# Memory keys and values kept on chip through the experts, and memory weights and rows loaded in longer runs

## The chip, the cores and the metric

The kernel runs on one core of one Trainium2 chip. A core has TensorE (matrix products), VectorE, ScalarE, GpSimd and SyncE, which here only issues loads, and 16 DMA engines that all queues share. The metric is the device time of one execution in microseconds (us), the median of the runs.

## The reference, cut to what matters

A first block (attention, a recurrent mixer, then a mixture of 32 experts) is followed by a second block of two layers on 256 tokens of width 1024. Both layers of the second block have attention over 256 memory rows, whose keys and values depend on inputs alone, not on the tokens:

```python
def memory_attention(qm, mem, w_mem_kv):
    B, M, _ = mem.shape
    km, vm = jnp.split(mem @ w_mem_kv, 2, axis=-1)
    km = km.reshape(B, M, MEM_HEADS, MEM_HEAD_DIM)
    vm = vm.reshape(B, M, MEM_HEADS, MEM_HEAD_DIM)
    lg = jnp.einsum('bshd,bmhd->bhsm', qm, km).astype(jnp.float32) * (MEM_HEAD_DIM ** -0.5)
    p = jax.nn.softmax(lg, axis=-1)
    o = jnp.einsum('bhsm,bmhd->bshd', p, vm)
    return o.reshape(qm.shape[0], qm.shape[1], MEM_W).astype(qm.dtype)
```

`mem` is 256 x 1024 and `w_mem_kv` 1024 x 512 for each layer, all in float32. Every expert has a gate and an up matrix of 1024 x 512 and a down matrix of 512 x 1024, 2 MB each. The kernel runs all 32 experts.

## The kernel before, in words

**Stages.** The first block's attention and mixer come first, then the router, then the experts, in 16 pairs (`DUOS`); then the first block's final normalization, the second block's first attention and FFN, and its second attention and FFN. The engines run programs of their own and meet at semaphores.

**The experts' loads.** A pair needs six units of 2 MB: two gate, two up, two down. Even pairs use the six slots of `ring`. Odd pairs use four spare places for gate and up (`spare`: one in `wide_rows` and `rowvec`, three in `arena`) and the ring for down. SyncE issues them in the order of use. Before each it waits until the unit's last reader is done (`used_up`: `moe["gate_up"]` or `moe["down"]`). An expert's unit is read in runs of 16 KB for each partition, or 8 KB where a unit comes in halves. Several loads are queued at a time.

**The memory's part.** Between the pairs, the keys and values of both layers are made. SyncE loads one memory weight matrix per layer (`mem_weights`, in the place of a gate unit: `mem_unit`) and the memory rows into `X`. TensorE turns the rows in 16 transposes (`mem_columns`, line 945), ScalarE puts them back into `X` as `memT` (line 2128), and TensorE makes keys and values (`mem_product`, through `product`, line 886) in banks 2 and 3, at 289 us for the first layer and 354 us for the second. Two gate loads, of pairs 4 and 6, go where the matrices lay and wait for these products (`first_unit_swapped`, line 807).

**Where the products go.** Their place in the second block, `km` and `vm`, is the end of `arena_and_mem`, which a spare unit uses until the last pair. So ScalarE copies each 512-column product in three pieces (`mem_out`, line 2136) into free places (`mem_stage`: 256 columns in `w_router`, 128 in `tri`, 128 in `wide_rows`), and GpSimd stores each piece to a tensor in device memory, `by_memory` (line 3153): 12 stores of 64 or 128 KB, 1 MB in all. The next product isn't copied until the stores of the one before have landed (`mem_stored`). After the last gate and up product SyncE loads all 1 MB into `km` and `vm` in one piece (line 863), between the loads of the second block's first weights; `mem_back` tells TensorE that they are there, before the memory's scores (line 1481).

**The end of the experts.** The last pair's units come in halves. The last product of gate and up (line 1242) is followed by ScalarE's silu (line 2108), VectorE's product (line 2669), transposes, and the down products (line 1260), the second half of which waits for the last load. VectorE then copies the result (line 2672), TensorE adds it (line 1269), ScalarE squares (line 2179), and VectorE normalizes into `X` (lines 2776 to 2780). TensorE turns `X` and ScalarE empties it into `wide_rows` (line 2091). `keep_awake` (line 892) issues products of zeros that write a bank nobody reads.

**After that.** SyncE loads in the order of `ring_units`: from the second block two parts of the attention input, then the stored products, then the third part, two compression matrices and the rest. Line 1671 and 1853 are the attention's products, line 1695 and 1745 the FFNs'. GpSimd makes sums for the FFNs (lines 3182 to 3187).

Of the kernel before, what the change touches and what calls it, by code (L numbers as in the profile page):

```python
# [14 lines left out]
F32 = mybir.dt.float32  # L15
# [7 lines left out]
P = 128  # L23
T = 256
# [247 lines left out]
def build(nc, x, meta_tokens, lb_logits, g_mix, w_in, sb_gain, hg_gain, w_out, g_ffn, w_router_group,  # L272
# [9 lines left out]
    with ExitStack() as ctx:  # L282
# [3 lines left out]
        def sem(name):  # L286
            return ctx.enter_context(nc.semaphore(name))
# [39 lines left out]
        def take(n, *dims):  # L327
# [99 lines left out]
        by_block = nc.dram_tensor("by_block", [HEADS, CMP_PAD, T], F32).ap()  # L427
        by_memory = nc.dram_tensor("by_memory", [P, UNIT // 2], F32).ap()
        mem_stage = [(0, MEM, w_router[:, :, :].rearrange("p k n -> p (k n)")[:, 0:MEM]), (MEM, P, tri[:, :]),
                     (MEM + P, P, wide_rows[:, 0:P])]  # L430
        expanded = sem("expanded")
# [6 lines left out]
        mem_in, mem_weights_in, mem_turned, mem_kept = sem("mem_in"), sem("mem_weights_in"), sem("mem_turned"), sem("mem_kept")  # L438
        mem_made, mem_staged, mem_stored, mem_back = sem("mem_made"), sem("mem_staged"), sem("mem_stored"), sem("mem_back")
        in_pack, in_pack1 = sem("in_pack"), sem("in_pack1")  # L440
# [191 lines left out]
        def _(sp):  # L632
# [96 lines left out]
            def used_up(u, pairs):  # L729
                sp.wait_ge(moe["down" if u >= 4 else "gate_up"], pairs * 2)  # L730
# [57 lines left out]
            def mem_weights(layer):  # L788

                used_up(0, 2 * layer + 2)  # L790
                src = kmaj((a_w_mem_kv_2, b_w_mem_kv_2)[layer][0])
                sp.dma_start(mem_unit(layer), src).then_inc(mem_weights_in, 16)

            mem_weights(0)
            for u in range(SPARES, 6):
                used_up(u, 2)
                next_unit(u, 2, False)
            sp.dma_start(X[:, :, :], mem_2[0].rearrange("(b p) d -> p b d", p=P)).then_inc(mem_in, 16)

# [59 lines left out]
            for u in (2, 1):  # L859
                load(second + u)  # L860
            used_up(1, DUOS)
            sp.wait_ge(mem_stored, 16 * 3 * 4)
            sp.dma_start(arena_and_mem[:, ARENA:ARENA + half_unit], by_memory).then_inc(mem_back, 16)
            for u in (0, 3, 4, 6, 9):
# [11 lines left out]
        def _(pe):  # L876
# [61 lines left out]
            def mem_columns():  # L938
                pe.wait_ge(mem_in, 16)
                for j in range(4):  # L940
                    if j >= 2:
                        pe.wait_ge(mem_kept, j - 1)
                    for r in range(2):
                        for tb in range(TB):
                            last = pe.transpose(bank[2 + j % 2][:, r * T + tb * P:r * T + (tb + 1) * P],
                                                X[:, tb, (2 * j + r) * P:(2 * j + r + 1) * P], ident[:, :])
                    last.then_inc(mem_turned, 1)
# [493 lines left out]
            def attend(layer):  # L1441
# [17 lines left out]
                def scores(together):  # L1459

                    _, kind, pair, _, _ = att[together[0]]
                    if kind == "mem":
                        wait_emptied(pe, "b_qm" if layer else "a_qm")
                        pe.wait_ge(mem_back, 16)
                    else:
                        wait_emptied(pe, "b_q" if layer else "a_q", pair // 2)
                        wait_emptied(pe, *(("b_k", pair // 2) if layer else ("a_kv", 1)))
# [429 lines left out]
        def _(act):  # L1897
# [233 lines left out]
            def mem_out(n):  # L2131
                act.wait_ge(mem_made, n + 1)
                if n:
                    act.wait_ge(mem_stored, 16 * 3 * n)
                for at, w, v in mem_stage:
                    last = act.activation(v, bank[2 + n % 2][:, at:at + w], ACT.Copy)
                last.then_inc(mem_staged, 1)
# [15 lines left out]
            for layer in range(2):  # L2153
                moe_quad(1 + layer, memory=layer)
            act.wait_ge(mem_stored, 16 * 3 * 4)
            with act.Fori(3, LAST_QUAD) as i:
# [27 lines left out]
            def empty_ln(name, layer, which):  # L2184
                at = PACK_ROWS + layer * LAYER_ROWS
                empty_normed(name, at + LAYER_PACK[f"ln{which}_g"][0], at + LAYER_PACK[f"ln{which}_b"][0], 2 * layer + which - 1)

            empty_normed("xTa", cols[:, PACK["g_final"][0]:PACK["g_final"][0] + KT], None)
            def attend(layer):
# [125 lines left out]
        def _(dve):  # L2315
# [458 lines left out]
            for tb in range(TB):  # L2774
                dve.wait_ge(y_squared, tb + 1)
                ts(sm(10 + tb, 1), sm(604 + 2 * tb, 1), 1.0 / D, EPS, ALU.mult, ALU.add).then_inc(stat_ready, 1)
                dve.wait_ge(sq_ready, 5 + 2 * tb)
                step(dve.reciprocal(sm(12 + tb, 1), sm(12 + tb, 1)))
                for n in range(2):
                    last = ts(X[:, tb, n * HALF:(n + 1) * HALF], bank[4 + 2 * tb + n][:, :], sm(12 + tb, 1), None, ALU.mult)  # L2780
                last.then_inc(normed, 1)
# [282 lines left out]
        def _(pool):  # L3064
# [82 lines left out]

            for n in range(4):
                layer, side = divmod(n, 2)
                pool.wait_ge(mem_staged, n + 1)  # L3150
                for at, w, v in mem_stage:
                    to = (2 * side + layer) * HALF + at
                    pool.dma_start(by_memory[:, to:to + w], v).then_inc(mem_stored, 16)
            pool.wait_ge(moe["down"], 2 * DUOS)
# [101 lines left out]
```

## Time and profile before

| what | value |
|---|---|
| median of 3 runs | 1387.59 us (1387.23 to 1391.06) |
| profiled execution, from first to last instruction | 1388.4 us |
| TensorE busy | 1219.2 us, 88% |
| VectorE, ScalarE, GpSimd busy | 469.4, 269.5, 327.3 us |
| moved by DMA | 337.94 MB, mean 243 GB/s |
| chain that ended last: TensorE, DMA | 71%, 18% |
| experts, first saturated load to last down product | about 237 to 675.6 us |
| granted clock of TensorE, mean | 0.942 |

The page gives one execution. Its span is all of it that the profile shows; no time outside the span is given. Busy shares are over the whole span; a stage with another limit has to be read by itself, in the stretches below. The chain goes back from the last instruction to what released it. "DMA share" is the mean busy share of the 16 engines, which can read slightly over 1 in a short stretch.

### The profile page before, as it was taken

Reading aid. Unit: us, or ns where it says so; the run is one execution under the profiler, and the core shown is the slowest. Engines: PE = TensorE matmul, PEld = TensorE weight load, DVE = VectorE, ACT = ScalarE, POOL = GpSimd, SP = SyncE. Lnnn points to the kernel's source line nnn. Section 1 sums busy time; section 2 is a strip of 40 time slices with the busy share of each in tenths; the row PEclk is TensorE's granted clock in tenths of the full one; section 3 lists DMA queues with packets and bytes.
Section 4 is the critical chain, followed back from the end, with each engine's and each line's share of the span. In section 5 each row is a group of like instructions: output and inputs, shape, how many; then the busy total and the mean of one; then the engine's idle time right before and its main releaser. Section 6 shows DMA issues by size and latency. Waiting matters only on the chain.

```text
span 1388.4 us, 18557 instructions
## 1 busy us (share of the span) xinstructions
PE 1219.2 (88%) x7567; PEld 795.4 (57%) x7567; DVE 469.4 (34%) x1160; ACT 269.5 (19%) x692; POOL 327.3 (24%) x348
## 2 busy tenths in 40 slices
PE   7999999985956566676898989999999999999997
PEld 6774555352512122231476559999448665999843
DVE  3352434101001010110213646444574214534467
ACT  4313432010000000000224532111003322111100
POOL 5000100000000000000100336878200113878800
PEclk9999999998978778888999999999999999999999
DMA  9643346999999999999984306544434038555400
GB/s 345 190 173 120 121 163 263 409 427 422 427 429 428 427 428 429 430 426 422 400 283 157 104 2 224 183 170 182 151 122 152 1 118 284 191 166 183 152 1 30
DMA packets 103102, 337.94 MB, mean 243 GB/s; under 512 B 6936, under 2 KB 58448, under 8 KB 88813
## 3 DMA queue, kind: packets, MB, share of 16 engines
q1 hardware_dynamic: 99958, 327.38, 61.3%
q0 software_dynamic: 2864, 9.35, 1.8%
q8 instruction: 59, 0.97, 0.3%
q14 instruction: 22, 0.18, 0.0%
q10 hardware_dynamic: 199, 0.06, 0.0%
HBM read 334.63 MB, written 3.91 MB: 244 GB/s over the span
## 4 chain that ended last, share of the span: by engine, by line
PE 71%; DMA 18%; DVE 4%; POOL 3%; ACT 2%; issue 2%; SPq 1%; POOLq 0%; DVEq 0%; ACTq 0%
PE bank L1695 18%; PE bank L886 17%; DMA ring<-in_w_expert_up 10%; PE bank L1745 8%; PE bank L1242 5%; PE bank L1260 4%; DMA ring<-in_w_expert_down 2%; DMA ring<-in_w_expert_gate 2%; DMA wide_rows<-in_w_expert_gate 2%; PE bank L1853 2%; PE bank L1132 2%; PE bank L1671 2%; PE bank L1521 1%; PE bank L1578 1%; PE bank L1269 1%
## 5 line engine op out<-in xcount | busy, mean ns | idle before, releaser
L886 PE MATMUL bank<-wide_rows,ring 128*128 128x256 f32 (+3 forms) x576 | 129.4, 377 | 1.9 <-DVE arena L2423 1.7
L1695 PE MATMUL bank<-R,arena 128*128 128x128 f32 x1056 | 125.1, 275 | 0.0
L1242 PE MATMUL bank<-ring,arena 128*32 128x512 f32 x512 | 77.6, 695 | 50.5 <-DMA ring<-in_w_expert_up 38.0
L1695 PEld LDWEIGHTS bank<-R,arena 128*128 128x128 f32 x1056 | 121.5, 192 | 0.0
L886 PEld LDWEIGHTS bank<-wide_rows,ring 128*128 128x128 f32 (+1 forms) x576 | 106.5, 193 | 23.0 <-issue 6.4
L1242 PE MATMUL bank<-wide_rows,arena 128*32 128x512 f32 x128 | 68.8, 689 | 49.1 <-DMA arena<-in_w_expert_up 36.2
L2669 DVE TENSOR_TENSOR arena<-arena,bank 64x512 f32<-64x512 f32 x16 | 11.1, 692 | 295.4 <-ACT arena L2108 295.4
L1695 PE MATMUL bank<-wide_rows,ring 128*128 128x128 f32 x704 | 91.2, 275 | 1.5 <-ACT wide_rows L2093 1.5
L1695 PEld LDWEIGHTS bank<-wide_rows,ring 128*128 128x128 f32 x704 | 84.7, 192 | 2.5 <-ACT wide_rows L2093 2.5
L1260 PE MATMUL bank<-ring,arena 128*32 128x512 f32 x504 | 72.5, 718 | 13.6 <-ACT arena L2111 10.1
L1745 PE MATMUL bank<-arena 128*128 128x512 f32 x176 | 81.4, 593 | 0.5 <-DVE arena L3032 0.5
L3171 POOL TENSOR_TENSOR arena<-arena,small 128x512 f32<-128x512 f32 (+1 forms) x44 | 38.0, 865 | 182.0 <-DVE small L2853 144.5
L1242 PEld LDWEIGHTS bank<-ring,arena 128*32 128x32 f32 x512 | 19.4, 126 | 98.3 <-issue 84.4
L3182 POOL TENSOR_TENSOR arena<-ring 128x512 f32<-128x512 f32 x44 | 56.6, 1286 | 77.2 <-PE bank L1695 56.9
L2108 ACT ACTIVATE arena<-bank 64x512 f32<-64x512 f32 x16 | 9.4, 588 | 329.1 <-PE bank L1242 329.1
L3146 POOL DMA_DIRECT2D wide_rows<-in_g_final x1 | 0.5, 538 | 304.1 <-PE bank L1260 304.1
L886 PE MATMUL bank<-ring,wide_rows 128*128 128x512 f32 (+2 forms) x192 | 71.8, 529 | 0.0
L1242 PEld LDWEIGHTS bank<-wide_rows,arena 128*32 128x32 f32 x128 | 14.7, 124 | 96.8 <-issue 80.4
L1242 PE MATMUL bank<-arena 128*32 128x512 f32 x384 | 67.0, 668 | 0.0
L1745 PE MATMUL bank<-ring,arena 128*128 128x512 f32 x132 | 62.4, 594 | 1.0 <-POOL arena L3209 1.0
L2999 DVE TENSOR_TENSOR arena<-arena,bank 128x128 f32<-128x128 f32 x44 | 12.6, 287 | 135.6 <-ACT arena L2273 135.6
L1745 PEld LDWEIGHTS bank<-arena 128*128 128x128 f32 x176 | 33.2, 190 | 42.9 <-issue 40.7
(383 smaller groups left out, 1990.3 us busy)
## 6 DMA issues: line engine op xcount, KB each, us to landing
ring<-in_w_expert_down SPq DMA_DIRECT2D x29, 2048.0 KB, 16.8
ring<-in_ffn_w_in SPq DMA_DIRECT2D x44, 1024.0 KB, 8.4
ring<-in_w_expert_gate SPq DMA_DIRECT2D x16, 2048.0 KB, 25.0
ring<-in_w_expert_up SPq DMA_DIRECT2D x16, 2048.0 KB, 33.1
arena<-in_w_expert_up SPq DMA_DIRECT2D x14, 2048.0 KB, 30.9
ring<-in_ffn_w_out SPq DMA_DIRECT2D x10, 2048.0 KB, 8.0
ring<-in_w_in SPq DMA_DIRECT2D x7, 2048.0 KB, 15.6
arena<-in_w_expert_gate SPq DMA_DIRECT2D x7, 2048.0 KB, 26.5
```

What stands on the lines that cost most here:

```text
L886: last = pe.matmul(dst, lhsT, rhs, start=k == 0, stop=k == len(pairs) - 1)
L1132: last = pe.matmul(b[:, :], mixT[:, k, tb * P:(tb + 1) * P], w[:, k, :], start=k == 0, stop=k == KT - 1)
L1242: last = pe.matmul(bank[e % 2][at:at + SLOTS, :], xg_tile(e % 2, k)[:, SLOTS * r:SLOTS * r + SLOTS], w[r][:, kk, :], start=k == 0, stop=k ...
L1260: last = pe.matmul(bank[e % 2][at:at + SLOTS, :], hidden_T[e % 2][:, f * DUO + SLOTS * r:f * DUO + SLOTS * (r + 1)], w[r][:, ff, n * HALF: ...
L1269: last = pe.matmul(bank[4 + 2 * tb + n][:, :], give[e % 2][half, tb * P:(tb + 1) * P], yrow[e % 2][half, :], start=False, stop=final)
L1521: last = pe.matmul(dst, v, p, start=k == 0, stop=k == len(lower[1]) - 1)
L1671: last = pe.matmul(b[:, :], headT[:, k, tb * P:(tb + 1) * P], w[:, k, :], start=k == PAIRS, stop=k == PAIRS - 1)
L1695: last = pe.matmul(up_banks[layer][u % 4][i][:, at * P:(at + 1) * P], weights(k), columns(k), start=k == 0, stop=k == KT // 2 - 1)
L1745: return pe.matmul(down_banks[layer][which][:, :], left, right, start=p == 0, stop=p == STEPS_F - 1)
L1853: last = pe.matmul(b[:, :], headT[:, k, tb * P:(tb + 1) * P], w[:, k, :], start=k == b_first[0], stop=k == b_last[-1])
L3171: pool.tensor_tensor(v, v, sm(684 + 8 * (u % LOGITS), 2).unsqueeze(2).broadcast_to([P, 2, w]), ALU.mult).then_inc(at_p, 1)
L3182: pool.tensor_tensor(s[0], b_low, b_high, ALU.add).then_inc(ph["w_sums"], 1)
```

## The change

1. The products stay on chip. `by_memory`, its 12 stores, its load and the semaphore `mem_stored` are gone. The first layer's products are staged by ScalarE in `w_router` and `ones` (keys) and in `tri`, `wide_rows` and `level_mask` (values), which nothing reads any more. The second layer's products go, in one instruction each and when both are made, into the first half of `X`, where `memT` is then no longer needed.
2. After the last gate and up product GpSimd copies all of it into `km` and `vm`, in seven copies of 256, 256, 512, 128, 128, 256 and 512 columns. `mem_back` is now set by the last of them. VectorE waits for it before the final normalization writes `X`, ScalarE before it writes `wide_rows`, TensorE before the memory's scores.
3. SyncE's waits for `used_up(1, DUOS)` and `mem_stored` are gone with the load.
4. Each partition gets two neighbouring rows of a memory weight matrix, 4 KB in one run instead of 2 KB, and two neighbouring memory rows, 8 KB instead of 4 KB. The transposes read every second column to match.

```diff
-        by_memory = nc.dram_tensor("by_memory", [P, UNIT // 2], F32).ap()
-        mem_stage = [(0, MEM, w_router[:, :, :].rearrange("p k n -> p (k n)")[:, 0:MEM]), (MEM, P, tri[:, :]),
-                     (MEM + P, P, wide_rows[:, 0:P])]
+        late_memory = X[:, 0, :].rearrange("p (a b c) -> p a b c", b=2, c=MEM)
+        mem_stage = [[(0, MEM, w_router[:, :, :].rearrange("p k n -> p (k n)")[:, 0:MEM]), (MEM, MEM, ones[:, 0:MEM])],
+                     [(0, P, tri[:, :]), (P, P, wide_rows[:, 0:P]),
+                      (MEM, MEM, level_mask[:, :, :].rearrange("p a b -> p (a b)").bitcast(F32))]]
...
                 used_up(0, 2 * layer + 2)
-                src = kmaj((a_w_mem_kv_2, b_w_mem_kv_2)[layer][0])
-                sp.dma_start(mem_unit(layer), src).then_inc(mem_weights_in, 16)
+                src = (a_w_mem_kv_2, b_w_mem_kv_2)[layer][0].rearrange("(j p r) n -> p j (r n)", p=P, r=2)
+                sp.dma_start(mem_unit(layer).rearrange("p (j r) n -> p j (r n)", r=2), src).then_inc(mem_weights_in, 16)
...
-            sp.dma_start(X[:, :, :], mem_2[0].rearrange("(b p) d -> p b d", p=P)).then_inc(mem_in, 16)
+            sp.dma_start(X[:, :, :], mem_2[0].rearrange("(p b) d -> p b d", p=P)).then_inc(mem_in, 16)
...
             for u in (2, 1):
                 load(second + u)
-            used_up(1, DUOS)
-            sp.wait_ge(mem_stored, 16 * 3 * 4)
-            sp.dma_start(arena_and_mem[:, ARENA:ARENA + half_unit], by_memory).then_inc(mem_back, 16)
             for u in (0, 3, 4, 6, 9):
                 load(second + u)
...
                         for tb in range(TB):
-                            last = pe.transpose(bank[2 + j % 2][:, r * T + tb * P:r * T + (tb + 1) * P],
-                                                X[:, tb, (2 * j + r) * P:(2 * j + r + 1) * P], ident[:, :])
+                            by_row = X[:, tb, j * MEM:(j + 1) * MEM].rearrange("p (f r) -> p r f", r=2)
+                            last = pe.transpose(bank[2 + j % 2][:, r * T + tb * P:r * T + (tb + 1) * P], by_row[:, r, :], ident[:, :])
...
-                        pe.wait_ge(mem_back, 16)
+                        pe.wait_ge(mem_back, 1)
...
             def mem_out(n):
-                act.wait_ge(mem_made, n + 1)
-                if n:
-                    act.wait_ge(mem_stored, 16 * 3 * n)
-                for at, w, v in mem_stage:
-                    last = act.activation(v, bank[2 + n % 2][:, at:at + w], ACT.Copy)
+                layer, side = divmod(n, 2)
+                if layer == 0:
+                    act.wait_ge(mem_made, n + 1)
+                    for at, w, v in mem_stage[side]:
+                        last = act.activation(v, bank[2 + side][:, at:at + w], ACT.Copy)
+                else:
+                    act.wait_ge(mem_made, 4)
+                    last = act.activation(late_memory[:, side], bank[2 + side][:, :].rearrange("p (b c) -> p b c", b=2), ACT.Copy)
                 last.then_inc(mem_staged, 1)
...
-            act.wait_ge(mem_stored, 16 * 3 * 4)
             with act.Fori(3, LAST_QUAD) as i:
...
+            act.wait_ge(mem_back, 1)
             empty_normed("xTa", cols[:, PACK["g_final"][0]:PACK["g_final"][0] + KT], None)
...
             for tb in range(TB):
                 dve.wait_ge(y_squared, tb + 1)
+                dve.wait_ge(mem_back, 1)
...
-            for n in range(4):
-                layer, side = divmod(n, 2)
-                pool.wait_ge(mem_staged, n + 1)
-                for at, w, v in mem_stage:
-                    to = (2 * side + layer) * HALF + at
-                    pool.dma_start(by_memory[:, to:to + w], v).then_inc(mem_stored, 16)
+            pool.wait_ge(mem_staged, 4)
+            pool.wait_ge(moe["gate_up"], 2 * DUOS)
+            for side, home in enumerate((km, vm)):
+                for at, w, v in mem_stage[side]:
+                    pool.tensor_copy(home[0].rearrange("p b c -> p (b c)")[:, at:at + w], v)
+                last = pool.tensor_copy(home[1], late_memory[:, side])
+            last.then_inc(mem_back, 1)
             pool.wait_ge(moe["down"], 2 * DUOS)
             load_rowvec(g_final)
```

## Rows read from the trace of the kernel before

**Rows 1.** Page, part 2: GpSimd and the DMA engines in 40 slices.

```profile
POOL 5000100000000000000100336878200113878800
...
DMA  9643346999999999999984306544434038555400
GB/s 345 190 173 120 121 163 263 409 427 422 427 429 428 427 428 429 430 426 422 400 283 157 104 2 224 183 170 182 151 122 152 1 118 284 191 166 183 152 1 30
```

**Rows 2.** Stretches of 237 to 675.6 us; last columns clock granted, DMA share, GB/s.

```profile
262.00:271.00 9.00, 8.46 (x72) 2.67 (x72) 1.48 (x5) 0.49 (x1) 0.00 (x0) 1.00 1.00 357
271.00:285.00 14.00, 9.43 (x66) 2.94 (x66) 0.69 (x1) 1.19 (x2) 0.00 (x0) 0.76 1.00 421
...
297.00:313.00 16.00, 15.51 (x103) 7.91 (x101) 0.00 (x0) 0.95 (x5) 3.24 (x6) 1.00 1.00 423
...
341.00:349.00 8.00, 5.53 (x44) 1.79 (x40) 0.69 (x1) 1.04 (x2) 0.00 (x0) 1.00 1.03 397
...
400.00:636.00 236.00, 149.09 (x1009) 55.40 (x1002) 20.70 (x48) 9.48 (x16) 0.00 (x0) 0.81 1.01 428
```

**Rows 3.** Waits, 237 to 676 us: total, times, longest.

```profile
PE bank L1242 <- DMA ring<-in_w_expert_up: 38.0, 4, 10.3
...
ACT w_router L2136 <- DMA by_memory<-wide_rows: 18.3, 2, 9.5
```

**Rows 4.** Chain that ended last, 237 to 420 us.

```profile
266.62 14.01 DMA ring<-in_w_expert_down
...
303.41 30.48 DMA wide_rows<-in_w_expert_gate
```

**Rows 5.** TensorE's waits for DMA from 676 us to the end.

```profile
PE bank L1260 <- DMA ring<-in_w_expert_down: 0.4, 1, 0.4
```

**Rows 6.** DMA packets in 297:313, 313:325, 361:380, 341:349 and 271:285.

```profile
q0 software_dynamic: 159, 0.39, 6.3%
...
q0 software_dynamic: 65, 0.13, 2.8%
...
q0 software_dynamic: 216, 0.52, 7.0%
...
DMA packets 1122, 3.18 MB, mean 397 GB/s; under 512 B 32, under 2 KB 32, under 8 KB 1056
...
DMA packets 600, 5.90 MB, mean 421 GB/s; under 512 B 48, under 2 KB 48, under 8 KB 304
```

**Rows 7.** Timeline of SyncE's queue, 240 to 700 us: start, length.

```profile
257.31 0.38 SPq L792 DMA_DIRECT2D wide_rows<-in_a_w_mem_kv  x1
266.25 0.80 SPq L727 DMA_DIRECT2D ring<-in_w_expert_down  x2
...
323.32 16.61 SPq L727 DMA_DIRECT2D arena<-in_w_expert_gate  x1
...
656.92 15.18 SPq L711 DMA_DIRECT2D ring<-in_a_w_in  x2
672.21 4.93 SPq L863 DMA_DIRECT2D arena<-by_memory  x1
```

**Rows 8.** GpSimd's groups by form: total, mean ns.

```profile
L3182 POOL TENSOR_TENSOR arena<-ring 128x512 f32<-128x512 f32 x44 | 56.6, 1286 | 77.2 <-PE bank L1695 56.9 <-DVE R L2866 20.3
...
L3106 POOL CAST level_mask<-arena 128x128 uint8<-128x128 f32 x7 | 2.0, 291 | 0.5
```

**Rows 9.** Timeline at the end of the experts.

```profile
669.99 0.69 DVE L2669 TENSOR_TENSOR arena<-arena,bank 64x512 f32<-64x512 f32 x1 [14.17 <-ACT arena L2108]
...
675.60 1.92 PE L1260 MATMUL bank<-ring,arena 128*32 128x512 f32 x16 [0.38 <-DMA ring<-in_w_expert_down]
...
680.23 0.15 DVE L2776 TENSOR_SCALAR small<-small 128x1 f32<-128x1 f32 x1 [1.95 <-ACT R L2179]
```

**Rows 10.** VectorE's line 2999 in the FFNs: minimum, median, maximum ns.

```profile
L2999 DVE TENSOR_TENSOR arena<-arena,bank x44: 277/288/289, 849.5 to 1312.0; 128x128 f32<-128x128 f32 x44
```

**Rows 11.** Transposes of the memory rows: minimum, median, maximum ns.

```profile
L945 PE MATMUL bank<-ident,X x16: 272/273/329, 286.1 to 288.3; 128*128 128x128 f32 x16
```

More of the change, by code:

```diff
@@ L438, in build @@
         mem_in, mem_weights_in, mem_turned, mem_kept = sem("mem_in"), sem("mem_weights_in"), sem("mem_turned"), sem("mem_kept")
-        mem_made, mem_staged, mem_stored, mem_back = sem("mem_made"), sem("mem_staged"), sem("mem_stored"), sem("mem_back")
+        mem_made, mem_staged, mem_back = sem("mem_made"), sem("mem_staged"), sem("mem_back")
         in_pack, in_pack1 = sem("in_pack"), sem("in_pack1")
```

## The prediction

> **What bounds the kernel now.** I read the page first, part 2. From the seventh to the nineteenth slice, which is where the experts are, the 16 DMA engines are 90% busy or more and move 400 to 430 GB/s [rows 1]. Cut into the experts' own stretches, the DMA share is 1.00 or a little above in every one, while TensorE is busy 149 of 236 us between 400 and 636 [rows 2]. The waits say it from the other side: in this stage TensorE waits for weights of the up matrices, 38.0 us in 4 waits on the ring alone [rows 3]. The chain of work agrees, with pieces of 14.01 and 30.48 us that are one expert load each [rows 4]. So from about 237 to 675.6 us the kernel is a stream of weights: a byte or a slow packet less in it moves the end of the experts forward, and nothing that TensorE, ScalarE or VectorE does less of in that time does. From 676 us to the end, TensorE waits for a DMA once, for 0.4 us [rows 5]. What is saved in transfers there has no price.
>
> The reader is to see where the stream is not at its plain rate. Between 400 and 636 us, experts alone, it is 428 GB/s. From 262 to 271 us it is 357, from 271 to 285 us 421, from 341 to 349 us 397 [rows 2]. The packets of those three stretches are the memory's: 1,056 of the 1,122 packets of 341 to 349 us are under 8 KB, 1,024 of them the 2 KB runs of one 2 MB memory weight matrix; in 271 to 285 us the excess is the 256 runs of 4 KB of the memory rows [rows 6].
>
> **Stores (removed).** Twelve stores on GpSimd's queue, 1 MB in all, lie inside the stream. Queue 0 took 6.3% of the 16 engines in 16 us, 2.8% in 12 us and 7.0% in 19 us [rows 6]: 1.01 + 0.34 + 1.33 = 2.68 us of the whole stream. By bytes it is (0.39 + 0.13 + 0.52) MB over 428 GB/s = 2.43 us. I take 2.6 us, ends 2.43 and 2.68. All of it counts, because loads are queued before and behind it. ScalarE's 18.3 us of waiting for the stores [rows 3] also goes, and counts for nothing: it stands under a TensorE that waits for loads afterwards.
>
> **Longer runs (changed).** The weight matrices go from 2 KB to 4 KB runs, the rows from 4 KB to 8 KB. The second matrix costs 8 us x (428 - 397)/428 = 0.58 us over the plain rate, with 1,024 packets. With 512 packets it is half, 0.29 us, if a packet has one fixed cost; the memory rows, whose 256 packets of 4 KB cost 14 us x (428 - 421)/428 = 0.23 us, say 0.46 us for 512 of 4 KB. The saving is therefore between 0.12 and 0.29 us; I take 0.2. The memory rows save 0 to 0.23 us, I take 0.1. The first matrix has the same packets but costs 9 us x (428 - 357)/428 = 1.49 us, 0.91 us more than the second. It was issued at 257.31 us with little queued, and the next load only at 266.25 us [rows 7], when TensorE was done with the down product; the second had six loads around it. Whether longer runs mend that 0.91 us no row shows. I take half, and so 0.2 + 0.45 = 0.65 us, ends 0.12 and 1.49. If the matrix lands sooner, the down weights issued at 266.25 us, which end the 14.01 us of the chain [rows 4], land sooner by as much.
>
> The Trainium skill, page DMA: Bandwidth & Descriptors, section Specifications, asks for 512 B a transfer as the least for full rate; by that, 2 KB runs are already long enough. The trace disagrees, with 397 against 428 GB/s. By the rule the three run terms would be nothing and the sum 2.6 us; by the rows it is more.
>
> **Load back (removed).** The 1 MB load of the stored products is issued at 672.21 us [rows 7], behind the last expert load, so it is no part of the stream that ends at 675.6 us. SyncE's queue stood 4.93 us in it; the loads of the second block that follow (the third part of the attention input and the two compression matrices) start about 5 us earlier. Nothing waited for those [rows 5], so this is 0. The cover is TensorE's work on the normalized rows and on the first parts of the attention input, which had landed. SyncE is also held 16.61 us behind the second memory matrix and 15.18 us at the first loads of the second block [rows 7]; fewer packets may end the first of these, but the DMA share stays 1.0 through it, so it is 0 too.
>
> **Copies on GpSimd (added).** Seven copies at the end of the experts, after the last gate and up product: 256, 256, 512 columns and 128, 128, 256, 512. The trace has no such copy. A 128-column cast takes 291 ns, a two-source sum of 512 columns 1,286 ns [rows 8]. As upper end, with half of the sum's time for 256 columns, 2 x 0.29 + 3 x 0.65 + 2 x 1.29 = 5.1 us. They can start before VectorE's last hidden product at 669.99 us, and the first instruction that waits for them is VectorE's at 680.23 us [rows 9]: a gap of 10.2 us, so 5.1 us are hidden. Behind that instruction stand the final normalization, TensorE's transposes and the whole second block, so beyond 10.2 us each us costs one. The two other waits (ScalarE's emptying into wide_rows, TensorE's memory scores) come later still. GpSimd has no other work: its next load, the final gain, waits for the last down product anyhow.
>
> VectorE's hidden product at 669.99 us now runs beside these copies. If it had to stand behind one, the last down half would be late by at most 1.29 - 0.38 = 0.9 us, 0.38 us being TensorE's idle time there [rows 9]. Against it: line 2999 has the same operands, one in the arena and one in a bank, and took 277 to 289 ns in 44 executions in the FFNs, where GpSimd is 70 to 90% busy with sums [rows 1, 10]. I take 0.
>
> **Moved and reordered.** The second layer's two products are copied out of their banks in one instruction each instead of three, the first of them only when both are made, about 7 us later. What waits for it is the gather, behind the pair's gate and up products, as before. Reading the memory rows with a step of two in the 16 transposes could make them dearer; they take 16 x 273 ns = 4.4 us by their durations [rows 11], and twice that is still inside one pair's wait, about 10 us [rows 3]. Price 0 for both.
>
> **The sum.** 2.6 + 0.2 + 0.1 + 0.65 = 3.55 us. Smallest: 2.43 + 0.12 + 0 + 0.12 = 2.67 us. The profiled span is 1388.4 us, 0.8 us above the median of the runs; nothing outside the span is shown, so the difference is taken from the median: 1387.59 - 3.55 = 1384.0 us. A measurement of this kernel tells about 0.3%, 4.2 us, from no change; the forecast lies just inside that.
>
> **Rivals.**
>
> *The stream gains more.* The memory loads run at the plain rate: 2.68 + 1.49 + 0.58 + 0.23 = 4.98 us, time 1382.6 us. For it: the first matrix's slow stretch is 2.6 times as dear as the second's with equal packets, so most of it isn't packet cost, and a shorter queue of packets may remove it. Against: the memory rows show that 4 KB packets aren't free.
>
> *Nothing is gained.* The stream is paced by when loads may be issued, not by its rate. The chain goes from TensorE's memory products into the load issued at 303.41 us [rows 4], and the one at 266.25 us too is released by TensorE. If the next buffers free no earlier, the removed stores leave gaps. The time is 1387.6 us. Against: the DMA share is 1.00 to 1.03 in every stretch [rows 2], and loads take 30 us to land, some six deep.
>
> *Slower.* GpSimd's copies hold the final normalization. They begin at 669.99 us at the latest and decide from 10.2 us on. To undo the gain they must take 10.2 + 3.55 = 13.8 us, and to be slower by over 0.3%, another 4.2 us, 17.9 us, or 2.6 us each, twice the dearest GpSimd row. The time is then above 1391.8 us.
>
> **How the numbers follow.** Forecast 0.62, more gained 0.15, nothing gained 0.15, slower or something unseen 0.08. The forecast's own range is 1382.6 to 1384.9 us, with the runs' spread on top. The 8 in 10 range is 1382.0 to 1387.8 us, which takes in the larger gain and most of no gain. Faster by over 0.3% means below 1383.4 us: 0.3 of the forecast and nearly all of the larger gain, 0.33. Slower 0.08, within 0.3% 0.59.
>
> **What would show it.** Right: queue 0 has no packets between 297 and 380 us; the last down product of the experts starts 3 to 4 us before 675.60; every later stage keeps its length; the seven copies end before VectorE's normalization; the stretch of the second memory matrix reads about 410 GB/s. Wrong: the DMA share drops below 1 near 266 or 303 us; VectorE's normalization waits for GpSimd; the time after the last down product changes; the end of the experts moves by less than 2.4 us.

## The result and the profile after

The first comparison gave 1381.33 us as the median of 7 executions (1379.6 to 1385.84) against 1388.82 us for the kernel before (7 executions, 1387.23 to 1391.66): ratio 0.9945, 95% interval 0.9927 to 0.9963. Forecast were 1384.0 us and a range of 1382.0 to 1387.8 us. So the change gained more than the range allowed. Two later comparisons on two chips, 12 executions of the changed kernel each, gave 0.9969 (0.9947 to 0.9990) and 0.9979 (0.9960 to 0.9998); the experiments below are about that difference.

The profiled execution after spans 1377.9 us and took 1379.6 us, 1.7 us more than its span; in every recorded execution it is 1.7 to 1.8 us. It is 10.5 us shorter than the profiled span before. Page, part 2, of after:

```profile
DMA  9643356999999999999974217544434048544400
GB/s 347 196 171 122 122 202 266 426 427 425 426 428 428 428 428 429 429 427 421 392 253 152 76 43 229 178 152 165 153 122 153 1 137 284 192 155 181 153 1 30
```

The stream is as full as in [rows 1]. Its slow stretches are where [rows 2] had them, some 5 to 8 us earlier and less slow. Stretches of after (busy time of the engines, then granted clock, DMA share, GB/s):

```profile
257.00:262.00 5.00, 3.76 (x36) 1.01 (x32) 0.69 (x1) 0.00 (x0) 0.00 (x0) 1.00 0.97 393
264.00:278.00 14.00, 9.46 (x63) 3.10 (x63) 0.69 (x1) 1.19 (x2) 0.00 (x0) 0.81 1.01 430
...
333.00:341.00 8.00, 5.87 (x44) 1.90 (x42) 0.69 (x1) 0.71 (x2) 0.00 (x0) 1.00 1.00 410
400.00:636.00 236.00, 149.57 (x1012) 55.78 (x1004) 20.71 (x48) 9.48 (x16) 0.00 (x0) 0.81 1.01 427
```

The second matrix, in runs of 4 KB, reads 410 GB/s in 8 us where it read 397 in runs of 2 KB, which is the figure forecast. The memory rows in runs of 8 KB read 430 against 421, but before_again reads 428 GB/s over the same work with the runs of 4 KB, so that these rates don't show a gain. The first matrix leaves a dip of 393 in 5 us where there were 357 in 9; the two windows aren't the same work, and the comparison from one starting point follows in the account of the prediction.

SyncE's queue of after, for [rows 7]:

```profile
250.62 0.38 SPq L793 DMA_DIRECT2D wide_rows<-in_a_w_mem_kv  x1
259.56 0.80 SPq L728 DMA_DIRECT2D ring<-in_w_expert_down  x2
...
317.89 0.50 SPq L728 DMA_DIRECT2D arena<-in_w_expert_gate  x1
318.44 5.38 SPq L728 DMA_DIRECT2D arena<-in_w_expert_up  x2
...
648.63 19.50 SPq L712 DMA_DIRECT2D ring<-in_a_w_in  x3
```

SyncE no longer stands 16.61 us behind the second matrix; it stands 5.38 us at a later load. The end of the experts in after, for [rows 9], with the first and the last of the seven copies:

```profile
660.66 0.40 POOL L3154 COPY arena<-w_router 128x256 f32<-128x256 f32 x1 [471.90 <-PE bank L1240]
...
661.17 0.69 DVE L2670 TENSOR_TENSOR arena<-arena,bank 64x512 f32<-64x512 f32 x1 [13.63 <-ACT arena L2106]
...
662.71 0.61 POOL L3155 COPY arena<-X 128x512 f32<-128x512 f32 x1
...
666.81 1.92 PE L1258 MATMUL bank<-ring,arena 128*32 128x512 f32 x16 [0.41 <-DMA ring<-in_w_expert_down]
...
671.44 0.15 DVE L2778 TENSOR_SCALAR small<-small 128x1 f32<-128x1 f32 x1 [1.95 <-ACT R L2179]
```

The copies run from 660.66 to 663.32 us and VectorE needs them at 671.44 us. VectorE's product beside them takes 0.69 us as before. The last down product starts at 666.81 instead of 675.60 us: 8.79 us of the 10.5 are there by then. How many of these belong to the experts? The two gate loads that open the full stream were issued at 237.80 us before and at 232.81 us after: 4.99 us were there before anything that the change touches. From that issue to the last down product it is 437.80 us before and 434.00 us after: 3.8 us. The last 1.7 us came in the second block.

The 6.7 us outside are the granted clock. Four stretches of before:

```profile
56.00:67.00 11.00, 10.70 (x39) 9.02 (x40) 0.76 (x2) 0.75 (x2) 2.46 (x3) 0.71 0.46 148
136.00:148.00 12.00, 12.00 (x42) 6.54 (x42) 2.03 (x7) 3.16 (x6) 0.00 (x0) 0.86 0.21 89
243.00:249.00 6.00, 6.00 (x40) 1.66 (x44) 0.61 (x1) 0.00 (x0) 0.00 (x0) 0.72 1.01 429
816.00:823.00 7.00, 6.79 (x32) 3.44 (x28) 0.42 (x1) 0.43 (x2) 0.68 (x1) 0.76 0.01 2
```

And where the same work is in after:

```profile
56.00:67.00 11.00, 10.99 (x58) 9.82 (x59) 2.42 (x5) 1.23 (x2) 2.46 (x3) 1.00 0.52 158
132.00:144.00 12.00, 12.00 (x54) 7.30 (x54) 2.61 (x9) 4.79 (x10) 0.00 (x0) 1.00 0.27 110
238.00:244.00 6.00, 6.00 (x56) 1.84 (x60) 0.69 (x1) 0.00 (x0) 0.00 (x0) 1.00 1.00 426
806.00:813.00 7.00, 5.72 (x34) 3.21 (x35) 0.91 (x3) 1.37 (x5) 1.69 (x2) 1.00 0.01 2
```

The clock column is 0.71, 0.86, 0.72 and 0.76 before and 1.00 in all four after: TensorE was at its lower level, 1.2 GHz, for part of each stretch. Before, the product of 32 instructions at 56 us takes 10.17 instead of 7.14 us, the one of 16 at 138 us 8.47 instead of 7.03 us, and the eight ahead of it 1.45 instead of 1.16 us: 4.8 of the 5.0 us that after is ahead when the stream begins. Around 816 us it is 5.10 instead of 3.63 us in the chain, most of the last 1.7 us. Either the change takes these drops away, or they fall by chance.

### The profile page after: what moved, and what is told of

Its sections match the earlier page's. It is cut to its first block, busy times and chain, and to the rows that moved or that the text cites. A ratio compares the mean times of both kernels' runs of the same rounds, so it can differ in the third digit from the quotient of the medians.

```text
span 1377.9 us, 18538 instructions
## 1 busy us (share of the span) xinstructions
PE 1210.1 (88%) x7559; PEld 791.4 (57%) x7567; DVE 469.1 (34%) x1160; ACT 269.0 (20%) x687; POOL 323.6 (23%) x343
## 4 chain that ended last, share of the span: by engine, by line
PE 71%; DMA 18%; DVE 4%; POOL 3%; ACT 2%; issue 2%; SPq 1%; POOLq 0%; DVEq 0%; ACTq 0%
PE bank L1693 18%; PE bank L884 17%; DMA ring<-in_w_expert_up 10%; PE bank L1743 8%; PE bank L1240 5%; PE bank L1258 3%; DMA ring<-in_w_expert_down 2%; DMA ring<-in_w_expert_gate 2%; PE bank L1851 2%; DMA wide_rows<-in_w_expert_gate 2%; PE bank L1130 2%; PE bank L1669 2%; PE bank L1519 1%; PE bank L1576 1%; PE bank L1267 1%
## 5 line engine op out<-in xcount | busy, mean ns | idle before, releaser
L884 PE MATMUL bank<-wide_rows,ring 128*128 128x256 f32 (+3 forms) x576 | 126.4, 371 | 1.9 <-DVE arena L2424 1.7
```

The lines of the kernel that those rows point to most:

```text
L884: last = pe.matmul(dst, lhsT, rhs, start=k == 0, stop=k == len(pairs) - 1)
```

## The experiments

Theory one: the change moves the experts' stretch by about 3 us and nothing else; the rest of the first 7.5 us is how the clock's drops fell in few executions. Theory two: the drops belong to the kernel before, and the change removes them too. A third reading gives the longer runs, not the stores, the larger part.

The measure for the stretch is in every profile: the issue of the two gate loads ("ring<-in_w_expert_gate x2") to the start of the last down product. The table has it, what lies ahead of it and behind it, all from one profiled execution each, and the medians of all executions of the comparison (that of before is shared by the kernels that ran on the same chip).

| kernel | ahead, us | stretch, us | behind, us | median, us (executions) | before beside it, us | ratio (interval) |
|---|---|---|---|---|---|---|
| before | 237.80 | 437.80 | 712.80 | | | |
| before_again | 238.75 | 437.00 | 711.25 | 1388.30 (12) | 1388.04 | 0.9999 (0.9983 to 1.0016) |
| before_third | 234.55 | 437.00 | 714.55 | 1386.98 (12) | 1387.91 | 0.9993 (0.9973 to 1.0012) |
| after | 232.81 | 434.00 | 711.09 | 1381.33 (7) | 1388.82 | 0.9945 (0.9927 to 0.9963) |
| after_again | 234.51 | 434.03 | 711.16 | 1384.73 (12) | 1388.18 | 0.9969 (0.9947 to 0.9990) |
| after_third | 239.22 | 433.87 | 711.01 | 1385.64 (12) | 1387.91 | 0.9979 (0.9960 to 0.9998) |
| runs_only | 234.79 | 436.18 | 709.53 | 1387.42 (12) | 1388.04 | 0.9994 (0.9978 to 1.0010) |
| onchip_only | 239.04 | 435.74 | 709.52 | 1384.95 (12) | 1388.04 | 0.9980 (0.9963 to 0.9997) |
| stores_doubled | 235.04 | 439.81 | 714.45 | 1392.43 (12) | 1388.18 | 1.0033 (1.0013 to 1.0052) |
| copies_sixfold | 239.37 | 433.92 | 720.11 | 1389.55 (10) | 1388.18 | 1.0009 (0.9987 to 1.0032) |
| kept_awake | 233.17 | 433.80 | 711.13 | 1384.76 (12) | 1388.18 | 0.9976 (0.9956 to 0.9995) |
| kept_awake_twice | 238.90 | 433.71 | 709.39 | 1382.20 (12) | 1387.91 | 0.9951 (0.9934 to 0.9969) |

Single executions of the kernel before range from 1382.6 to 1395.0 us, 124 in all, with a standard deviation of 3.0 us. The profiles of before and of onchip_only have a clock drop inside the stretch, near 244 us. Before's stretch is 437.80 - 437.00 = 0.8 us longer with it; these two are compared with each other, the rest with 437.00.

**before_again**: the kernel before, unchanged.

> The kernel before, once more, to see how its own executions scatter. Theory one (the drops of the granted clock outside the experts fall by chance): its profile shows drops at other places than 56, 136, 243 and 816 us, or none, and its span moves by 2 to 7 us with them; time 1387 to 1391 us, ratio 1.000. Theory two (the drops belong to the kernel before, and the change takes them away): the same four stretches at 0.71 to 0.86 of the clock again, in the same places, and never a time under 1385 us.

The stretches of before, read again in before_again:

```profile
56.00:67.00 11.00, 10.95 (x51) 9.57 (x52) 0.74 (x2) 0.61 (x2) 2.47 (x3) 0.84 0.49 156
136.00:148.00 12.00, 12.00 (x52) 6.80 (x50) 2.78 (x9) 5.09 (x11) 0.72 (x1) 1.00 0.08 31
243.00:249.00 6.00, 5.31 (x50) 1.68 (x53) 0.69 (x1) 0.60 (x1) 0.00 (x0) 1.00 1.01 429
816.00:823.00 7.00, 6.22 (x43) 3.71 (x44) 0.42 (x1) 1.20 (x3) 0.87 (x1) 1.00 0.01 2
```

Three of the four drops are gone and one is shorter, in the same code. The execution isn't much shorter for it, 1387.0 us of span, because there is a long drop at 224 to 232 us instead. Its fastest execution took 1384.3 us, under the 1385 us that theory two had set. Theory two falls in its strong form.

**runs_only**: the kernel before with the longer runs alone.

```diff
-                src = kmaj((a_w_mem_kv_2, b_w_mem_kv_2)[layer][0])
-                sp.dma_start(mem_unit(layer), src).then_inc(mem_weights_in, 16)
+                src = (a_w_mem_kv_2, b_w_mem_kv_2)[layer][0].rearrange("(j p r) n -> p j (r n)", p=P, r=2)
+                sp.dma_start(mem_unit(layer).rearrange("p (j r) n -> p j (r n)", r=2), src).then_inc(mem_weights_in, 16)
...
-            sp.dma_start(X[:, :, :], mem_2[0].rearrange("(b p) d -> p b d", p=P)).then_inc(mem_in, 16)
+            sp.dma_start(X[:, :, :], mem_2[0].rearrange("(p b) d -> p b d", p=P)).then_inc(mem_in, 16)
```

(with the transposes' strided reads, as in the change)

> Only the longer runs of the memory weights and rows. My sum: 0.95 us less in the experts' stretch (0.2 to 2.3), time some 1388 us. A rival that gives the runs the larger part (the first matrix's slow stretch gone): 2 us or more. If the load's packets steer where the clock falls, also some us outside the experts; by chance alone, nothing steady.

The stretch is 436.18 us, 0.8 us less. The median, 0.6 us less, can't be told from none. The rival of 2 us or more falls.

**onchip_only**: the changed kernel with both `rearrange` edits and the transposes as before.

> Only the products kept on chip, runs of 2 and 4 KB as before. My sum: 2.6 us less in the experts' stretch (2.4 to 2.7), time some 1386 us; nothing after the experts. The rival that nothing is gained by stores: 0. If the change as a whole takes 7.5 us by a part of its own outside the experts, it is this one or the runs alone that shows 4 us or more outside.

The stretch is 435.74 us, against 437.80 us with the same drop inside: 2.1 us less, somewhat under the 2.4 to 2.7 us expected. A second difference of the same kind, runs_only against the changed kernel and both without the drop, is 436.18 - 434.0 = 2.2 us. The median is 3.1 us less.

**stores_doubled**: the kernel before with a second copy of each store.

```diff
+        by_memory_too = nc.dram_tensor("by_memory_too", [P, UNIT // 2], F32).ap()
...
                     pool.dma_start(by_memory[:, to:to + w], v).then_inc(mem_stored, 16)
+                    pool.dma_start(by_memory_too[:, to:to + w], v).then_inc(mem_stored, 16)
```

(the waits for `mem_stored` count to twice as much)

> The kernel before with each of the 12 stores issued twice, the second time to another tensor. If stores are paid at the stream's rate, 1 MB more costs 2.4 to 2.7 us in the experts' stretch and in the time. If the stores lay in gaps (the rival that nothing is gained): 0. If they hold ScalarE's copies and through them TensorE: more than 3 us.

The stretch is 439.81 us, 2.8 us more; the median 4.2 us more, ratio 1.0033 (1.0013 to 1.0052). ScalarE's waits for the stores grew from 18.3 to 28.1 us, and TensorE's longest wait for the copies behind them is 1.1 us. The first six stores lengthen the way to the wait behind them by 1.7 us, all twelve the way to the next by 2.8 us. One MB of stores in the full stream costs 2.1 us when taken away and 2.8 us when added; the forecast's 2.6 us is between. Waits for GpSimd's stores in stores_doubled (total, times, longest):

```profile
ACT w_router L2137 <- DMA by_memory_too<-wide_rows: 28.1, 2, 15.0
```

**after_again** and **after_third**: the changed kernel, unchanged, on two chips.

> The changed kernel, once more, on another chip. If the experts' stretch is all that the change moves (about 3.4 us there, from the profiles) and the rest of the first 7.5 us was how the clock's drops fell in seven executions: a difference of 3 to 5 us to the kernel before, ratio 0.997, and drops outside the experts at 56, 216 to 232 and 740 us in this profile too. If the change does 7.5 us: ratio 0.9945 again and no drop at 56 us.

> The changed kernel, a third profile. The experts' stretch 434.0 us, 3.0 us less than before's; outside it no steady difference; time 3 to 4 us under before's. If a second effect outside the experts is real, the medians differ by 5 us or more again.

The stretch is 434.03 and 433.87 us, as in the first profile 434.00: it hardly scatters. Outside it, after_third lost at 56, 128 and 180 us what after had not:

```profile
56.00:67.00 11.00, 10.68 (x49) 9.34 (x50) 0.78 (x2) 0.87 (x2) 2.46 (x3) 0.84 0.47 147
128.00:133.00 5.00, 5.00 (x25) 1.81 (x26) 1.00 (x5) 1.47 (x6) 0.00 (x0) 0.66 0.00 0
180.00:184.00 4.00, 3.73 (x15) 2.37 (x14) 2.24 (x4) 1.02 (x5) 0.00 (x0) 0.57 0.64 217
```

Its part ahead of the stream is 239.22 us, the longest of the three and longer than before's. The medians are 3.4 and 2.3 us under those of before. The mean of these 24 executions is 3.3 us under the mean of the 124 of before (resampled interval 2.1 to 4.6 us); for the first 7 it is 6.0 us (4.0 to 7.8). Drawn from the 24 later executions, a median of 7 as low as 1381.33 us comes up in about 2 of 100 resamplings, so chance is a possible reading of the first comparison and not a comfortable one.

The record says more, because it gives the mean granted clock of each execution. In the 117 executions of before that have one, 0.001 more of mean clock goes with 1.1 us less. Against that line the changed kernel is 2.6, 2.4 and 1.6 us shorter in its three comparisons, each with a standard error of 0.5 to 0.6 us: at the same clock the first comparison gained hardly more than the second. What sets it apart is its mean clock, 0.9467 against 0.9450 and 0.9444 later and 0.9436 in before. (A shorter stream raises the mean clock a little by itself, as the experts' stretch, 0.81 between 400 and 636 us, lies under the mean.)

**before_third**: the kernel before, a third profile.

> The kernel before, a third profile, to see what of its length is fixed. From the profiles so far: from the issue of the two gate loads to the start of the last down product 437.0 us (437.8 with a clock drop at 244 us), whatever the execution; up to that issue 235 to 239 us, and after the last down product 709 to 714 us, by where the clock's drops fall. If instead the stretches outside are fixed in this kernel and longer than the changed one's, the change has a second effect.

The stretch is again 437.00 us, as in before_again. Its three "ahead" values, 237.80, 238.75 and 234.55 us, overlap with after's 232.81, 234.51 and 239.22. "Behind" it, before has 712.80, 711.25 and 714.55 us, the changed kernel 711.0 to 711.2 us three times. These differences are again the granted clock. Summed over windows of 2 us, TensorE was at its lower level between 676 and 830 us for about 7 us in the three profiles of the changed kernel and in before_again (711.0 to 711.3 us behind), for 10 us in before (712.80), for 14 us in before_third and stores_doubled (714.55 and 714.45), and for 3 us in runs_only and onchip_only (709.53 and 709.52). For the same time at the lower level, kernels with and without the change agree within 0.3 us, so the profiles leave no room for more than that by a second effect on the work itself. Whether it makes drops rarer is open: of the five profiles with the load back in them, two have a drop near 680 us (before_third and stores_doubled) and one near 816 us (before); none of the six without it has either, if copies_sixfold, which holds TensorE there, is left out.

**copies_sixfold**: the changed kernel with its seven copies made six times over.

```diff
+            for again in range(6):
+                if again:
+                    step(last)
-            for side, home in enumerate((km, vm)):
+                for side, home in enumerate((km, vm)):
```

> The changed kernel with its seven copies on GpSimd made six times over. One set took 2.7 us in the profile of after and had 10.8 us. Six take 16 us. If they are hidden up to 10.8 us and then hold the normalization one for one: 5.2 us slower than after. If the copies also hold VectorE's hidden product or its row copy beside them, more than 6 us, and that product is longer than 0.69 us or starts late.

The end of the last copy and VectorE's normalization:

```profile
682.94 0.62 POOL L3158 COPY arena<-X 128x512 f32<-128x512 f32 x1
...
683.68 0.15 DVE L2778 TENSOR_SCALAR small<-small 128x1 f32<-128x1 f32 x1 [7.71 <-POOL arena L3158]
```

The first copy began at 667.17 us, so six sets took 16.4 us. The last down product was at 673.29 us; in after, VectorE's instruction comes 4.63 us behind it, which would be 677.92 us here. It comes at 683.68 us, 5.8 us later, against 5.2 expected. VectorE's hidden product beside the copies took 0.69 us, so the copies hold nothing but the last wait. The part behind the experts is 9.0 us longer than in after, though, and not 5.8: while the normalization waits, TensorE stands idle (6.50 us ahead of the transposes), and its granted clock reads 0.50 from 682 to 692 us, where the transposes and the next product run. From the normalization to the product after these it is 1.6 us longer than in after (14.47 against 12.83 us), so in this execution the wait of 5.8 us cost 7.4. The other 1.6 us come later, where there is a drop near 822 us like before's near 816 us. The median is 4.8 us over that of after_again in the same comparison. This is the mechanism of the slower rival, and it takes some four sets of copies before it begins.

**kept_awake**: the changed kernel with seven products of zeros in TensorE's idle 1.7 us before 56 us.

```diff
                 elif what == "dist":
                     distances(i)
+                    if i:
+                        keep_awake(7, 7)
```

> The changed kernel with seven products of zeros in TensorE's idle 1.7 us before 56 us, which nobody reads. If that idle time is what lets the clock fall there in some executions, whatever the change: no drop at 56 us here, and a median 0.5 to 2 us under the changed kernel's. If the drops come from elsewhere: the same drop at 56 us and no difference.

No drop at 56 us in this profile, but the first profile of after had none there either, and the median is the same as after_again's, 1384.76 and 1384.73 us. Inconclusive for the time. As to the drop, nine of the ten profiles without these products have one at 56 us, and of the two with them (this one and the next) neither has; but kept_awake_twice has drops at 126 and 178 us instead, as after_third had at 128 and 180 us.

**kept_awake_twice**: the same, and ten more products of zeros before the compressed scores.

```diff
                 elif what == "cmp_l":
+                    to_fill(pe, "cmp_l", 0)
+                    keep_awake(10, jobs.bank("cmp_l", 0))
                     wait_emptied(pe, "cmp_kv")
```

> The changed kernel with the seven products of zeros before 56 us and ten more in TensorE's idle 2.4 us before the compressed scores (line 1647), which every profile so far has, with a granted clock at half for some 8 us behind it. If the idle time is what lets the clock fall, that drop goes in every execution, and the compressed scores take 2.2 instead of 4.4 us and the product behind them 7.1 instead of 8.9 us: 3 to 4 us less than the changed kernel, about 1381 us, and less scatter. If the clock falls there for another reason: the same time as the changed kernel.

In after, the stretches around the compressed scores, and TensorE's scores themselves:

```profile
732.00:736.00 4.00, 3.61 (x22) 3.61 (x22) 1.17 (x4) 1.97 (x4) 0.00 (x0) 0.69 0.00 0
736.00:740.00 4.00, 4.00 (x20) 2.58 (x21) 3.26 (x11) 0.36 (x1) 0.00 (x0) 0.50 0.00 0
```

```profile
732.39 4.36 PE L1647 MATMUL bank<-arena 128*128 128x32 f32 x24 [2.43 <-ACT arena L2246]
736.68 8.90 PE L1576 MATMUL bank<-wide_rows,ring 128*64 128x256 f32 x64
```

In kept_awake_twice:

```profile
740.00:744.00 4.00, 4.00 (x26) 2.76 (x27) 3.26 (x11) 0.36 (x1) 0.00 (x0) 0.68 0.00 0
744.00:748.00 4.00, 4.00 (x36) 2.58 (x34) 2.03 (x8) 0.36 (x1) 0.00 (x0) 0.90 0.00 0
```

```profile
738.20 2.87 PE L1651 MATMUL bank<-arena 128*128 128x32 f32 x24 [0.16 <-ACT arena L2250]
741.00 8.81 PE L1578 MATMUL bank<-wide_rows,ring 128*64 128x256 f32 x64
```

The scores take 2.87 instead of 4.36 us, but the clock still falls behind them, and the next product takes 8.81 us as before. Against after, scores and product are 1.6 us shorter. The same is seen without any products of zeros, in onchip_only:

```profile
740.37 3.19 PE L1647 MATMUL bank<-arena 128*128 128x32 f32 x24 [2.43 <-ACT arena L2246]
743.49 8.43 PE L1576 MATMUL bank<-wide_rows,ring 128*64 128x256 f32 x64
```

The two together took 11.6 us in runs_only, in onchip_only and here, 13.2 us in seven profiles and 14.8 to 14.9 us in two. So not "every profile so far", as written above, had the long drop, and one profile can't tell whether filling the idle time shortened it. The forecast that the drop goes in every execution is wrong, as it is there in this one. The time is another matter: 1382.20 us is 3.4 us under after_third in the same comparison, by the means 3.5 us (resampled interval 1.6 to 5.4 us), against 3 to 4 us expected, and the ratio to before is 0.9951 (0.9934 to 0.9969). The two sets of products of zeros together gain; by which drops, one profile doesn't show.

## Why the prediction was right and where it was wrong

**The stream (right, a little too large).** The sum was 3.55 us in the experts' stretch. It is 3.0 us between the profiles without a drop in the stretch (two of before at 437.00 us, three of the changed kernel at 433.87 to 434.03 us), and 3.8 in the first pair with 0.8 us of clock drop on the side of before. It came where it was said. Counted from the gate loads' issue, the three waits of the chain ended, in before_again, at 42.63, 95.36 and 160.76 us, and in after_again at 42.45, 93.90 and 157.73 us. So 0.2 us were gained by the first, 1.5 by the second (behind the first six stores), 3.0 by the third (behind the other six and the second matrix), and nothing after, 3.0 us at the end.

**Stores, 2.6 us.** 2.1 to 2.2 us by removal, 2.8 us by doubling: one under and one over the bounds of 2.43 and 2.68 us that were worked out from bytes and from engine time. Why removing gives less than adding costs is open.

**Longer runs, 0.95 us.** Together 0.8 us, but not by the terms. In runs_only the three waits ended at 42.29, 94.95 and 159.99 us, so 0.34 us earlier than in before_again behind the first matrix, 0.41 behind the memory rows, 0.77 behind the second matrix; before_third differs from before_again by 0.1 us in them. The rows gave some 0.1 us, as forecast. The second matrix gave 0.36 us where 0.2 was taken and 0.29 was the upper end, though its 410 GB/s were forecast. The term that was mis-sized most is the first matrix's, 0.65 us: it gave 0.34 us.

Its price was read from a profile that a clock drop had touched. The drop at 243 to 249 us made TensorE late with the down product, so that the loads behind the matrix were issued 28.45 us after the gate loads (28.43 in onchip_only); in every profile without that drop, of either kernel, it is 26.7 to 26.8 us. The 9 us that read 357 GB/s in [rows 2] begin 24.2 us after the gate loads' issue. The same 9 us in onchip_only (with the drop), before_again, runs_only and after:

```profile
263.24:272.24 9.00, 8.47 (x72) 2.66 (x72) 1.47 (x5) 0.47 (x1) 0.00 (x0) 1.00 1.02 362
262.95:271.95 9.00, 7.89 (x64) 2.33 (x56) 0.69 (x1) 0.00 (x0) 0.00 (x0) 1.00 1.02 388
258.99:267.99 9.00, 7.95 (x64) 2.34 (x56) 0.69 (x1) 0.00 (x0) 0.00 (x0) 1.00 1.01 413
257.01:266.01 9.00, 7.76 (x64) 2.33 (x56) 0.69 (x1) 0.00 (x0) 0.00 (x0) 1.00 1.01 417
```

In before_third it is 399. By the prediction's own formula the first matrix costs 9 x (428 - 388)/428 = 0.84 us in before_again and 0.61 us in before_third, close to the second's 0.58 us, instead of 1.49 us. Most of the 0.91 us, half of which was taken as mendable by longer runs, was thus the late issue. The rival "loads are paced by their issue" shows in the two profiles with the drop and in no other; even there the DMA share read 1.00 and 1.02, and the bytes told what the share didn't.

**Load back, SyncE's waits, ScalarE's waits: 0.** Right as far as the profiles show. SyncE's 16.61 us went and the chain of the second block didn't move against the end of the experts, but for the clock.

**Copies: 0.** Right. They took 2.7 us, half of the upper end of 5.1 us, and copies_sixfold shows the cover. Beyond it "each us costs one" was too cheap in the one execution profiled: 7.4 us for 5.8 us of wait, with the lower clock behind it. VectorE's product took 0.69 us beside six sets as beside one.

**The step that failed** is the one that put the rest of the execution at nothing ("every later stage keeps its length") and drew the range from it: "the forecast's own range is 1382.6 to 1384.9 us, with the runs' spread on top". The runs' spread wasn't put on top. I had three executions over 3.8 us and gave the lower end 0.6 us. Single executions scatter with a standard deviation of 3.0 us, so medians of 7 do by about 1.5 us. That the profiled span held at least four stretches of a clock under 0.9 outside the experts' waits was there to be read, and I read the mean clock only where TensorE waited for loads. A second sign was that the profiled execution's own time isn't its span: it is 1.7 us more in every record, so before's profile was of an execution of about 1390.1 us, 2.5 us above the median, and not 0.8.

What the runs showed in its place: of the 10.5 us between the first two profiles, 3.0 us are the stream and 0.8 us a drop inside it; 6.7 us are drops of the granted clock outside it. By the prediction's own signs two came out as wrong (the last down product started 8.8 us earlier and not 3 to 4, and the time after it changed by 1.7 us), and both for the clock, while the signs of the mechanism came out as right: no packets of queue 0, 410 GB/s, copies that end 8.1 us before they are needed.

Of the first 7.5 us between the medians, 3.0 us are the stream, shown by profiles and by both halves of the change. The rest goes with a higher mean clock in those 7 executions, and with before's 7, whose mean lay 0.9 us above that of all 124; the 24 later ones give 3.3 us. Why the clock of the first 7 was higher, by the draw or by something in that comparison, is open. One slip of reading changed nothing: the slices at 90% or more in [rows 1] are the eighth to the twentieth, and not the seventh to the nineteenth.

## What to carry to other kernels

In a stage whose DMA share is 1.0, price a transfer by its bytes over the stream's plain rate, and check it by the queue's own share of the engines; here the two gave 2.43 and 2.68 us where 2.1 and 2.8 were measured. Before pricing a slow stretch by its rate, look whether a drop of the granted clock just ahead of it made the next load late, or read the stretch in a second profile: 357 GB/s became 388 and 399. Before giving a range, look at the granted clock over the whole span and at more than three executions: a change of 3 us can't be told from 7 in one comparison of a kernel whose clock drops come and go, while the length of one DMA-bound stretch, from one issue to one product, told it to some 0.2 us from a single profile without a clock drop in it.

## What the runs showed of the hardware that I had not expected

- The same code, profiled three times, was granted the lower clock outside its long waits at 56, 136, 218, 244 and 816 us once, at 56 and 223 to 233 us the next time, and at 56, 216 and 680 us the third time; the drops near 740 us and near 1384 us were in all three, that near 740 us with different lengths. TensorE had been idle 1.7 us ahead of the one at 56 us, in executions with the drop and without it (7.14 us for the product behind it in after, 10.17 us in before).
- Filling an idle time of 2.4 us with products of zeros didn't remove the drop behind it: it began 3.2 us after the scores did in kept_awake_twice and 1.1 us after them in after, but 2.4 us after them in onchip_only, which has no filling.
- A clock drop went with lost time in a stage bound by DMA too: in before TensorE was 1.7 us late with a product that releases a load, the load was issued 1.7 us later, and the stage was 0.8 us longer (437.80 against 437.00 us).
- The rate of the saturated stream went by run length: 397 GB/s over 8 us with 2 MB in 2 KB runs, 410 GB/s with 4 KB runs, 428 GB/s with the experts' 16 KB runs. The Trainium skill, page DMA: Bandwidth & Descriptors, section Specifications, names 512 B as the least for full rate; here 2 KB fell short of it.
- On GpSimd a float32 copy took 0.30, 0.40 and 0.61 us for 128, 256 and 512 columns, under half of the 1.29 us of a two-source sum of 512 columns.
